# Shared keys of layer 1: their heads scaled on ScalarE, both cosine products ahead of both sums

## The chip, the cores and the metric

The kernel is one program on one core of a Trainium2 chip. The metric is the device time of one execution, in microseconds (us). Five engines work beside each other, each through its own queue, in program order: TensorE (PE in the rows; its weight loads are PEld), VectorE (DVE), ScalarE (ACT), GpSimd (POOL) and SyncE (SP), which only issues DMAs. They wait for each other by semaphores.

## What is computed

The reference is two transformer layers with a context stream, and then a block of another architecture. The change lies in the second layer (layer 1, the "odd" one), between the projection by `od_w_in` and its attention. Cut to what matters there:

```
p = a @ w_in                              # a: 256 latent and 256 context tokens
ck, cv, dk, dv = split(p_kv)              # ck: 2 heads of 64 shared by 8 query heads
ck = rms_norm(split_heads(ck, 2), ck_g)   # x * rsqrt(mean(x*x) + EPS) * g, per head
ck = apply_rope(ck, cos, sin)             # latent tokens only
out = window_gqa(cq, ck, cv, ck_ctx, cv_ctx, sink)   # attention, every query head needs all of ck
```

`window_gqa` is the first half of the attention stage, and `diff_attention_latent` (dq, dk, dv) the second.

## The kernel before, in words

Tokens lie in four tiles of 128: t = 0 and 1 are latent, t = 2 and 3 context. All float32 products are made of a high and a low half ("hi" and "lo"). A weight tile (128 x 2048) comes by DMA into a slot, ScalarE writes its high half (`feed` in the ScalarE program, line 1610), VectorE its low half (`feed` in the VectorE program, line 2212), and TensorE reads both (lines 933 to 935, three matmuls for each product).

The projection of the shared keys and values gives one bank of PSUM for each of the four token tiles, `("od", "ckv", t)`, with keys in columns 0 to 127 (two heads) and values in columns 128 to 255. For each key tile these steps follow:

1. ScalarE squares it (`odd_square`, line 1876).
2. VectorE sums the squares by head and makes the mean (`odd_means`, lines 2376 and 2289).
3. GpSimd raises it to the power -1/2 (`rsqrt`, line 3403).
4. VectorE scales the two heads with it (`odd_scale` to `head_scale`, line 2384): event `hn`.
5. For t = 0 and 1 VectorE makes the cosine product (line 2819), GpSimd the sine product (line 3480, event `orp`), and VectorE adds both (line 2836, event `orot`). For t = 2 and 3 there is only VectorE's product with the gain (line 2824, event `orot`).
6. TensorE turns the tile (`head_turn`, line 939), ScalarE writes the high half (line 1665, `ohi`), VectorE the low half (line 2284, `olo`).

The value half of the bank is copied by ScalarE (`odd_value`, line 1881, event `cv2`), which also gives the bank free. Before that copy ScalarE waits for `hn` of the tile.

The order on each engine is written by hand:

- ScalarE: the four squares; one exponential of two numbers for the lambda of the differential heads (line 1921, the first exponential after many Silu); then values and high halves of the keys in turn, `odd_value(0)`, `odd_value(1)`, `odd_hi(0)`, `odd_value(2)`, `odd_hi(1)`, and so on. `odd_hi(0)` feeds a weight tile first: the high half of the tile for the next pair of projections (`whi__62`). Then it squares the first pair, `dq`.
- VectorE: means 0; means 1, scale 0, rotate 0; means 2, scale 1, rotate 1; means 3, scale 2, rotate 2; scale 3, rotate 3; the four low halves of the keys; means of the pair `dq`; the low half of that weight tile (`wlo__61`).
- GpSimd: power 0, sine product 0, power 1, sine product 1, power 2, power 3.
- TensorE: 16 steps of the paired projections (`paired`), turns the four key tiles, then starts the attention stage `attend("a1")`: the scores of a head (lines 1191 to 1193), followed by more steps of the paired projections. Every unit of this stage waits for `ohi` and `olo` of all four key tiles and for all four values.

The scratch tiles of the change: `XN` (scaled keys, `odd__179` and `odd__180` in the rows), `XR` (`odd__181` to `184`), `XT` (sine products, `odd__185` and `186`), `SQ` (squares, `odd__187` and `188`), `CV` (values, `odd__172`), `CK3` (halves of the keys, `odd__170` and `171`). `XN`, `XT` and `SQ` have two buffers each, so tile t + 2 waits for tile t.

Of the kernel before, what the change touches and what calls it, by code (L numbers as in the profile page):

```python
# [15 lines left out]
ACT = mybir.ActivationFunctionType  # L16
# [104 lines left out]
class Count:  # L121
# [18 lines left out]
    "norm_a": ("nsq", "xn_a", "ntm_a", "nhi", "msq", "mxn", "mxh", "mx_a", "r0", "upon"),  # L140
    "root": ("nrs", "hrs", "lrs", "mrs", "prs"),
    "head_v": ("hrd", "hms", "hn", "qg", "qlo", "ocos", "orot", "olo", "dv_v", "v_v"),
    "head_a": ("hsq", "qhi", "ohi", "cv2", "dv_a", "v_a"),
    "conv_v": ("cu", "cw", "cv", "clo"), "conv_a": ("cg", "chi"),
    "att_v": ("neg", "pmix", "ptc_v", "fw", "fy", "flo"), "att_a": ("exp", "ptc_a", "fwe", "fhi"),
    "mod_v": ("grow", "spr", "stq_lo", "msum", "gsum", "gcp"), "mod_a": ("silu", "stq_hi", "cb"),
# [13 lines left out]
class Book:  # L160
# [6 lines left out]
    def did(self, name, *key, by=1):  # L167
        sem = SEM_OF.get(name, name)
        self.now[sem] += by
        if self.counting and not self.repeat:  # L170
            assert (name, *key) not in self.at, (name, key)
            assert self.by.setdefault(sem, self.engine) == self.engine, (name, sem)
            self.at[name, *key] = sem, self.now[sem]
        assert self.at[name, *key] == (sem, self.now[sem]), (name, key)
        return self.sems.get(sem), by
# [109 lines left out]
def _build(nc, ctx, I, cst_d, scr_d, out_d, packed):  # L285
    W = {name: Weight(name, SHAPES[name]) for name in WEIGHTS}
    book = Book()
    did = book.did
# [115 lines left out]
    XN, XR, XT, SQ = A3.some(2, 512), A3.some(4, 512), A3.some(2, 512), A3.some(2, 512)  # L404
# [90 lines left out]
    def bank(*key):  # L495
        return PS[bank_of[key]]
# [11 lines left out]
    SSN = [SM[:, 80 + 8 * i:88 + 8 * i] for i in range(8)]  # L508
# [72 lines left out]
    ODD_UNITS = [("cq", 0), ("cq", 1), *[("ckv", t) for t in range(4)], *PAIRS[0:6]]  # L581

    rotated = {("orp", *key) for key in ODD_UNITS if (key[2] == 0 if len(key) == 3 else key[1] < 2)}

    def turned_kind(kind, *at):
        return ("ck" if kind == "ckv" else kind, *at)
# [1011 lines left out]
    def scalar_program(e):  # L1598
        at = dict(tile=0, due=Due(book), gate="", ahead=2, slots={0, 1, 2, *slot_e})

        def due(*events):
            return at["due"](*events)
# [247 lines left out]
        for blk in range(2):  # L1850
            for f0 in range(0, 11, 2):
                m = min(2, 11 - f0)
# [17 lines left out]
        def odd_square(*key):  # L1870
            w_ = 128 if key[0] == "ckv" else 512
            feed(("prod", "od", *key))
            c = ODD_UNITS.index(key)
            for s, n in due(("prod", "od", *key), *([("hrd", *ODD_UNITS[c - 2])] if c > 1 else normed_lo("o", 1))):
                e.wait_ge(s, n)
            e.activation(SQ[c % 2][:, 0:w_], bank("od", *key)[:, 0:w_], ACT.Square).then_inc(*did("hsq", *key))

        def odd_value(t):
            for s, n in due(("hn", "ckv", t)):
                e.wait_ge(s, n)  # L1880
            e.activation(CV[:, t, :], bank("od", "ckv", t)[:, 128:256], ACT.Copy).then_inc(*did("cv2", t))
            empties(("od", "ckv", t), ("cv2", t))
# [27 lines left out]
        for t in range(2):  # L1910
# [3 lines left out]
            for o in range(2):  # L1914
                r = slice(64 * o, 64 * o + 64)
                e.activation(CQ4[t][r, :, o, :], v3(bank("ht", "cq", t), 4)[r], ACT.Copy).then_inc(*did("ohi", "cq", t, o))
        for t in range(4):
            odd_square("ckv", t)
        for s, n in due(("lam_s",)):
            e.wait_ge(s, n)  # L1920
        e.activation(LM[:, 2:4], LM[:, 0:2], ACT.Exp).then_inc(*did("lam_e"))
# [159 lines left out]
        for n_ in range(6):  # L2081
# [5 lines left out]
            for t in range(2):  # L2087
                if n_ >= 4:
                    if t:
                        for s, n in due(("prod", "s", n_, t), ("nrs", "s", t)):  # L2090
                            e.wait_ge(s, n)
                        e.activation(VA[:, t, (n_ - 4) * 384:(n_ - 3) * 384], bank("s", n_, t)[:, 0:384], ACT.Copy,
                                     scale=SS[:, t:t + 1]).then_inc(*did("sv_a", n_, t))
                        empties(("s", n_, t), ("sv_a", n_, t))
                    continue
                c = 2 * n_ + t
                for s, n in due(("prod", "s", n_, t), ("nrs", "s", t),
# [3 lines left out]
                             scale=SS[:, t:t + 1]).then_inc(*did("sx", n_, t))  # L2101
# [20 lines left out]
        for hf in range(2):  # L2122
            for t in range(2):
                feed(("prod", "uq", hf, t))
                for s, n in due(("prod", "uq", hf, t), ("score", "a2", 23, 0)):
                    e.wait_ge(s, n)
                m = e.activation(QTMS[t][:, hf * 384:(hf + 1) * 384], bank("uq", hf, t)[:, 0:384], ACT.Copy,
                                 scale=96 ** -0.5)
# [43 lines left out]
        for f0 in range(0, 32, 2):  # L2172
            c = f0 // 2
# [8 lines left out]
        past = []  # L2182
        for t in range(2):
            for half in range(2):
                post_square("mlp", half, t, bank("mlp2", t, half), JK, 16, ("prod", "mlp2", t, half), *past)
                past = [("psq", "mlp", half, t)]


    def vector_program(e):
        at = dict(tile=0, due=Due(book), gate="", chain=0, ahead=2, sums=0, slots={0, 1, 2, *slot_e}, begun=None, owed=[])  # L2190

        def due(*events):
            return at["due"](*events)
# [509 lines left out]
        for half in range(2):  # L2703
# [4 lines left out]
            for t in range(4):  # L2708
                feed(("prod", "o", 0, half, t))
                c = half * 4 + t  # L2710
# [36 lines left out]
        for blk in range(2):  # L2747
            for f0 in range(0, 11, 2):
                m = min(2, 11 - f0)
# [42 lines left out]
        def odd_means(*key):  # L2792
            w_, nh, c, _ = odd_unit(*key)
            head_means(key, nh, 64, SQ[c % 2], SSN[c % 8])

        def odd_scale(*key):
            w_, nh, c, (xn, _, _) = odd_unit(*key)
            past = [("orot", *turned_kind(*ODD_UNITS[c - 2]))] if c > 1 else [*normed_lo("o", 1)]
            head_scale(key, bank("od", *key)[:, 0:w_], nh, 64, SSN[c % 8], xn, ("prod", "od", *key), *past)
            if key[0] != "ckv":  # L2800
                empties(("od", *key), ("hn", *key))

        def odd_rotate(*key):
            odd_cosine(*key)
            odd_sum(*key)

        def odd_cosine(*key):
            w_, nh, c, (xn, xr, xt) = odd_unit(*key)
            g = dict(cq=0, ckv=1, dq=2, dk=3)[key[0]]
            heads = lambda x: x.rearrange("p (h f) -> p h f", f=64)  # L2810
            wide = lambda x, n: x.rearrange("p (o f) -> p o f", o=1).broadcast_to([128, n, 64])
            past = [("ht", *turned_kind(*ODD_UNITS[c - 4]))] if c > 3 else []
            for s, n in due(("hn", *key), ("tab",), *past):
                e.wait_ge(s, n)
            if ("orp", *key) in rotated:
                pair = range(2) if len(key) == 3 else (key[1],)
                for o, t in enumerate(pair):
                    x = slice(o * w_ // len(pair), (o + 1) * w_ // len(pair))
                    m = e.tensor_tensor(heads(xr[:, x]), heads(xn[:, x]),
                                        wide(TC[:, (g * 2 + t) * 64:(g * 2 + t) * 64 + 64], nh // len(pair)), ALU.mult)  # L2820
                m.then_inc(*did("ocos", *key))
            elif key[0] == "ckv":
                gain_ = GAIN[:, g * 64:(g + 1) * 64].rearrange("p (a o f) -> p a o f", a=1, o=1).broadcast_to([128, 2, 2, 64])
                e.tensor_tensor(twice(XR[c % 4]), spread_heads(xn), gain_, ALU.mult).then_inc(*did("orot", *turned_kind(*key)))
            else:
                e.tensor_tensor(heads(xr), heads(xn), wide(GAIN[:, g * 64:(g + 1) * 64], nh),
                                ALU.mult).then_inc(*did("orot", *turned_kind(*key)))
# [62 lines left out]
        for t in range(2):  # L2890
# [3 lines left out]
                low("olo", ("cq", t, o), CQ4[t][other, :, o, :], v3(bank("ht", "cq", t), 4)[r], CQ4[t][r, :, o, :],  # L2894
                    ("ohi", "cq", t, o))
            empties(("ht", "cq", t), ("olo", "cq", t, 1))
        for t in range(5):
            if t < 4:
                odd_means("ckv", t)
            if t:  # L2900
                odd_scale("ckv", t - 1)
                odd_rotate("ckv", t - 1)
        at["ahead"] = 0
        for t in range(4):
            odd_lo("ck", t, CK3, 2)
# [23 lines left out]
        for t, k0 in ((0, 0), (1, 4)):  # L2929
            for s, n in due(("mt", k0), ("gain", "n2b", 0), ("prod", "o", 1, 1, 1)):  # L2930
                e.wait_ge(s, n)
            for k in (k0, k0 + 1):
                m = e.tensor_scalar(XT32[:, k, :], bank("mt", k0)[:, (k - k0) * 256:(k - k0) * 256 + 256],
                                    sc2b[:, 2 * k:2 * k + 1], None, ALU.mult)
# [3 lines left out]
        for t in range(2):  # L2938
            for s, n in due(("router", t), ("mrs", t), ("r0",)):
                e.wait_ge(s, n)  # L2940
            m = e.scalar_tensor_tensor(out=LG[:, t * 8:t * 8 + 8], in0=bank("router", t)[:, 0:8], scalar=SS[:, t:t + 1],
                                       in1=R0, op0=ALU.mult, op1=ALU.add)
# [8 lines left out]
        for t in range(2):  # L2951
            m = e.max(MX[:, eight(t)], LG[:, eight(t)])
# [11 lines left out]
        for t in range(2):  # L2964
            m = e.tensor_scalar(SELR[:, eight(t)], iot, one(IX, t, 0), None, ALU.is_equal)
# [3 lines left out]
        for t in range(2):  # L2969
            m = e.scalar_tensor_tensor(out=SELR[:, eight(t)], in0=iot, scalar=one(IX, t, 1), in1=SELM[:, eight(t)],  # L2970
                                       op0=ALU.is_equal, op1=ALU.add)
# [208 lines left out]
        for n_ in range(6):  # L3180
# [5 lines left out]
            for t in range(2):  # L3186
# [8 lines left out]
                c = 2 * n_ + t  # L3195
# [169 lines left out]
    def gpsimd_program(e):  # L3365
# [99 lines left out]
        for c, key in enumerate(ODD_UNITS):  # L3465
            w_, g = (128, 1) if key[0] == "ckv" else (512, dict(cq=0, dq=2, dk=3)[key[0]])
            for c_, unit in [(0, ODD_UNITS[0]), (1, ODD_UNITS[1])] if c == 0 else [(c, key)] if c > 1 else []:
                rsqrt("hrs", unit, SSN[c_ % 8][:, 0:w_ // 64], ("hms", *unit))
            if ("orp", *key) in rotated:
                pair = range(2) if len(key) == 3 else (key[1],)  # L3470
                for s, n in due(("hn", *key), ("tab",)):
                    e.wait_ge(s, n)
                for o, t in enumerate(pair):
                    x = slice(o * w_ // len(pair), (o + 1) * w_ // len(pair))
                    nh = w_ // len(pair) // 64
                    x4 = XN[c % 2][:, x].rearrange("p (h q r f) -> p h q r f", h=nh, q=2, r=2)
                    t4 = XT[c % 2][:, x].rearrange("p (h q r f) -> p h q r f", h=nh, q=2, r=2)
                    for r in range(2):
                        tab = TS5[:, g, t, :, r, :].rearrange("p (o q) f -> p o q f", o=1).broadcast_to([128, nh, 2, 16])
                        m = e.tensor_tensor(t4[:, :, :, r, :], x4[:, :, :, 1 - r, :], tab, ALU.mult)  # L3480
                m.then_inc(*did("orp", *key))
# [142 lines left out]
```

## Time and profile before

| what | us |
|---|---|
| median of 3 runs | 1751.19 |
| lowest and highest | 1749.59 and 1753.67 |
| the profiled execution | 1750.59 |
| its span by the profile | 1748.8 |
| TensorE busy | 1649.5 |
| VectorE busy | 1233.2 |
| ScalarE busy | 835.9 |
| GpSimd busy | 163.5 |

The rows further below are of one profiled execution, with times from the start of its span. A row of a timeline has the start, the duration of the group, the engine, the line of the kernel, the operation, output and inputs with shapes, the count, and in brackets how long the engine had been idle before it and what is held to have released it. A short idle time can be named after the wrong engine where two ended at nearly the same moment. The granted clock of TensorE ("PEclk") is 1.00 at 2.4 GHz and 0.50 at 1.2 GHz.

### The profile page before, as it was taken

To read this page: it belongs to the slowest core of one execution; us is meant where nothing else is said; L and a number is where in the kernel's file an instruction comes from. 1 tells how busy PE (TensorE), PEld (TensorE's weight loads), DVE (VectorE), ACT (ScalarE), POOL (GpSimd) and SP (SyncE) were. 2 spreads that over 40 slices of the span, in tenths; PEclk is the share of its full clock that TensorE was granted. 3 is DMA by queue.
4 is the path that set the end of the run, shared out by engine and by line. 5 is a ranking of instruction groups with operands and counts; after the bars stand their busy time and mean duration, and the time that the engine had idled before them with its cause. 6 is when DMAs were issued, how large, how long until landed. Compare 5 with 4: busy or idle time off the path is not lost. (4 is left out here: it accounts for less than half of the span.)

```text
span 1748.8 us, 21453 instructions
## 1 busy us (share of the span) xinstructions
PE 1649.5 (94%) x8697; PEld 1405.3 (80%) x8697; DVE 1233.2 (71%) x1598; ACT 835.9 (48%) x1023; POOL 163.5 (9%) x157
## 2 busy tenths in 40 slices
PE   5999999999999999799899999999889989889998
PEld 2778877888888888697788788888779878779986
DVE  6488864587575545776689888998977666766644
ACT  6444433322122315344567777677655444555532
POOL 2110102000210023410200000002300000000000
PEclk9999989999999999898999999999999999999999
DMA  8443433355565423211479898898866622245553
GB/s 335 111 168 122 146 120 121 142 196 197 224 237 193 166 104 102 73 49 49 169 254 345 299 374 316 320 355 300 299 239 206 216 69 101 89 152 185 179 193 119
DMA packets 60505, 333.61 MB, mean 191 GB/s; under 512 B 14690, under 2 KB 15009, under 8 KB 28400
## 3 DMA queue, kind: packets, MB, share of 16 engines
q1 hardware_dynamic: 54640, 311.06, 49.0%
q0 software_dynamic: 4032, 14.57, 2.7%
q10 hardware_dynamic: 1728, 6.54, 1.0%
q8 instruction: 72, 1.18, 0.3%
q14 instruction: 33, 0.27, 0.0%
HBM read 331.00 MB, written 1.13 MB: 190 GB/s over the span
## 5 line engine op out<-in xcount | busy, mean ns | idle before, releaser
L2212 DVE TENSOR_TENSOR wlo__61<-raw__60,whi__62 128x2048 fp32r<-128x2048 f32 (+2 forms) x64 | 144.1, 2252 | 71.8 <-ACT whi__62 L1610 71.6
L2212 DVE TENSOR_TENSOR wlo__65<-raw__64,whi__66 128x2048 fp32r<-128x2048 f32 (+3 forms) x64 | 139.8, 2185 | 64.8 <-ACT whi__66 L1610 64.8
L1610 ACT ACTIVATE whi__62<-raw__60 128x2048 fp32r<-128x2048 f32 (+2 forms) x64 | 119.0, 1859 | 91.3 <-DMA raw__60<-in_ffn_w 43.1
L1610 ACT ACTIVATE whi__66<-raw__64 128x2048 fp32r<-128x2048 f32 (+3 forms) x64 | 115.4, 1803 | 70.7 <-DMA raw__64<-in_ffn_w 31.0
L2212 DVE TENSOR_TENSOR wlo__69<-raw__68,whi__70 128x2048 fp32r<-128x2048 f32 (+4 forms) x50 | 109.2, 2183 | 23.9 <-ACT whi__70 L1610 23.9
L3403 POOL TENSOR_TENSOR keep__58<-keep__58,keep__59 128x1 f32<-128x1 f32 (+3 forms) x48 | 53.4, 1116 | 601.8 <-DVE keep__58 L2289 601.7
L2248 DVE SCALAR_TENSOR_TENSOR wsum__71<-raw__68,silu_rows 128x1024 f32<-128x1024 f32 x84 | 100.0, 1220 | 1.4 <-DMA raw__68<-in_ada_w 0.8
L1610 ACT ACTIVATE whi__70<-raw__68 128x2048 fp32r<-128x2048 f32 (+4 forms) x50 | 90.5, 1810 | 17.1 <-DMA raw__68<-in_w_ff 11.8
L2212 DVE TENSOR_TENSOR wlo__237<-raw__236,whi__238 128x2048 fp32r<-128x2048 f32 (+1 forms) x24 | 51.3, 2138 | 10.1 <-ACT whi__238 L1610 9.9
L2508 DVE TENSOR_REDUCE keep__58<-ps 128x1 f32<-128x256 f32 (+1 forms) x88 | 44.5, 517 | 13.6 <-PE ps L1194 4.9
L2212 DVE TENSOR_TENSOR wlo__233<-raw__232,whi__234 128x2048 fp32r<-128x2048 f32 (+1 forms) x24 | 50.5, 2106 | 1.8 <-ACT whi__234 L1610 1.7
L933 PE MATMUL ps<-ffn__129,wlo__61 128*128 128x512 f32 (+1 forms) x128 | 47.5, 371 | 4.4 <-DVE ffn__130 L2284 2.7
L935 PE MATMUL ps<-ffn__129,whi__62 128*128 128x512 f32 (+1 forms) x128 | 47.0, 367 | 0.0
L934 PE MATMUL ps<-ffn__130,whi__62 128*128 128x512 f32 (+1 forms) x128 | 47.0, 367 | 0.0
L1610 ACT ACTIVATE whi__234<-raw__232 128x2048 fp32r<-128x2048 f32 (+1 forms) x24 | 42.5, 1771 | 8.5 <-DMA raw__232<-in_moe_w 8.4
L2248 DVE SCALAR_TENSOR_TENSOR wsum__147<-raw__144,silu_rows 128x1024 f32<-128x1024 f32 x36 | 44.3, 1251 | 0.4
L3501 POOL TENSOR_TENSOR moe__212<-moe__212,keep__57 128x512 f32<-128x512 f32 x2 | 11.4, 5686 | 351.2 <-DVE moe__213 L3077 343.6
L2212 DVE TENSOR_TENSOR wlo__241<-raw__240,whi__242 128x2048 fp32r<-128x2048 f32 (+2 forms) x24 | 43.2, 1798 | 1.2 <-ACT whi__242 L1610 1.2
L933 PE MATMUL ps<-ffn__129,wlo__141 128*128 128x512 f32 x112 | 43.6, 389 | 0.0
L934 PE MATMUL ps<-ffn__130,whi__142 128*128 128x512 f32 x112 | 43.6, 389 | 0.0
L935 PE MATMUL ps<-ffn__129,whi__142 128*128 128x512 f32 x112 | 43.6, 389 | 0.0
L933 PE MATMUL ps<-ffn__129,wlo__65 128*128 128x512 f32 x112 | 43.6, 389 | 0.0
(1173 smaller groups left out, 5331.0 us busy)
## 6 DMA issues: line engine op xcount, KB each, us to landing
raw__68<-in_moe_w SPq DMA_DIRECT2D x24, 1024.0 KB, 5.4
raw__60<-in_moe_w SPq DMA_DIRECT2D x24, 1024.0 KB, 5.7
raw__68<-in_ada_w SPq DMA_DIRECT2D x16, 1024.0 KB, 4.9
raw__64<-in_moe_w SPq DMA_DIRECT2D x16, 1024.0 KB, 5.5
raw__232<-in_moe_w SPq DMA_DIRECT2D x16, 1024.0 KB, 6.6
raw__236<-in_moe_w SPq DMA_DIRECT2D x16, 1024.0 KB, 7.2
raw__144<-in_ada_w SPq DMA_DIRECT2D x13, 1024.0 KB, 6.2
raw__68<-in_ada_w POOLq DMA_DIRECT2D x20, 512.0 KB, 4.1
```

The costliest lines, as they stand in the source:

```text
L933: e.matmul(out, ll, rh, start=start, stop=False)
L934: e.matmul(out, lh, rl, start=False, stop=False)
L935: return e.matmul(out, lh, rh, start=False, stop=stop)
L1610: e.activation(t.hi(), t.raw(), ACT.Copy).then_inc(*did("hi", i))
L2212: e.tensor_tensor(t.lo(), t.raw(), t.hi().bitcast(F32), ALU.subtract).then_inc(*did("lo", i))
L2248: m = e.scalar_tensor_tensor(out=junk, in0=slot_raw[t.slot][:, c * 1024:c * 1024 + 1024], scalar=1.0, in1=CB[:, v * D:(v + 1) * D], op0=AL ...
L2508: m = e.tensor_reduce(neg, b[:, 0:u.total], AX.X, ALU.max, negate=True)
L3403: e.tensor_tensor(x, x, EXPO[:, 0:1].broadcast_to([128, n_]) if n_ > 1 else EXPO[:, 0:1], ALU.pow).then_inc(*did(out, *key))
L3501: e.tensor_tensor(MACC[t][:, hs], MACC[t][:, hs], GBC[:, gs], ALU.mult).then_inc(*did("hgate", t, half))
```

## The change

ScalarE scales the heads of the four shared key tiles, one activation with a scale from memory for each head of 64 columns, in place of VectorE's one instruction for both. The scaled event is now `hna`, on ScalarE; VectorE's and GpSimd's products wait for it, and so does the copy of the values. On ScalarE the four scalings stand among the four squares, and thus ahead of the exponential at line 1921 and of all that follows it. On VectorE the order becomes: means 0, means 1, cosine 0, cosine 1, sum 0, means 2, sum 1, means 3, and the two products with the gain. GpSimd's and TensorE's order stays.

```diff
-    "head_a": ("hsq", "qhi", "ohi", "cv2", "dv_a", "v_a"),
+    "head_a": ("hsq", "hna", "qhi", "ohi", "cv2", "dv_a", "v_a"),
...
+    def head_normed(*key):
+        return ("hna" if key[0] == "ckv" else "hn", *key)
...
+        def odd_scale(t):
+            c = ODD_UNITS.index(("ckv", t))
+            for s, n in due(("hrs", "ckv", t), ("prod", "od", "ckv", t), ("orot", *turned_kind(*ODD_UNITS[c - 2]))):
+                e.wait_ge(s, n)
+            for h in range(2):
+                x = slice(h * 64, h * 64 + 64)
+                m = e.activation(XN[c % 2][:, x], bank("od", "ckv", t)[:, x], ACT.Copy, scale=SSN[c % 8][:, h:h + 1])
+            m.then_inc(*did("hna", "ckv", t))
+
         def odd_value(t):
-            for s, n in due(("hn", "ckv", t)):
+            for s, n in due(("hna", "ckv", t)):
...
-        for t in range(4):
-            odd_square("ckv", t)
+        for t in range(5):
+            if t < 4:
+                odd_square("ckv", t)
+            if t:
+                odd_scale(t - 1)
         for s, n in due(("lam_s",)):
             e.wait_ge(s, n)
         e.activation(LM[:, 2:4], LM[:, 0:2], ACT.Exp).then_inc(*did("lam_e"))
...
-            for s, n in due(("hn", *key), ("tab",), *past):
+            for s, n in due(head_normed(*key), ("tab",), *past):
...
-        for t in range(5):
-            if t < 4:
-                odd_means("ckv", t)
-            if t:
-                odd_scale("ckv", t - 1)
-                odd_rotate("ckv", t - 1)
+        for t in range(2):
+            odd_means("ckv", t)
+        for t in range(2):
+            odd_cosine("ckv", t)
+        for t in range(2):
+            odd_sum("ckv", t)
+            odd_means("ckv", 2 + t)
+        for t in range(2, 4):
+            odd_cosine("ckv", t)
...
-                for s, n in due(("hn", *key), ("tab",)):
+                for s, n in due(head_normed(*key), ("tab",)):
```

## Rows read from the trace of the kernel before

**Rows 1.** The page's first part: busy time, share, instructions of each engine.

```profile
PE 1649.5 (94%) x8697; PEld 1405.3 (80%) x8697; DVE 1233.2 (71%) x1598; ACT 835.9 (48%) x1023; POOL 163.5 (9%) x157
```

**Rows 2.** Windows: stretch, length, busy (instructions) of PE, PEld, DVE, ACT, POOL, clock, DMA.

```profile
713.30:716.50 3.20, 0.73 (x2) 0.30 (x2) 3.12 (x4) 0.48 (x1) 2.21 (x1) 0.60 0.00 0
716.50:720.80 4.30, 4.25 (x20) 4.28 (x21) 3.09 (x8) 0.83 (x3) 3.29 (x5) 0.50 0.02 4
...
806.00:809.00 3.00, 2.61 (x11) 2.29 (x13) 2.01 (x6) 1.94 (x5) 0.00 (x0) 0.52 0.02 5
...
815.00:818.00 3.00, 3.00 (x16) 2.43 (x15) 2.25 (x5) 1.21 (x4) 0.00 (x0) 0.78 0.13 52
```

**Rows 3.** The timeline of TensorE at the start of the attention stage.

```profile
708.10 0.41 PE L939 MATMUL ps<-keep__49,odd__183 128*128 128x128 f32 x2
709.92 0.44 PE L939 MATMUL ps<-keep__49,odd__184 128*128 128x128 f32 x2 [1.42 <-DVE odd__184 L2836]
...
713.40 0.47 PE L1191 MATMUL ps<-odd__171,odd__164 128*128 128x512 f32 x1 [1.02 <-ACT odd__187 L1876]
...
716.55 0.55 PE L933 MATMUL ps<-whi__62,odd__175 128*128 128x256 f32 x1 [2.42 <-DVE wlo__61 L2212]
```

**Rows 4.** The timeline of ScalarE in the same stretch.

```profile
705.81 0.28 ACT L1876 ACTIVATE odd__188<-ps 128x128 f32<-128x128 f32 x1
706.11 1.28 ACT L1921 ACT_TABLE_LOAD   x1
...
707.51 0.26 ACT L1881 ACTIVATE odd__172<-ps 128x128 f32<-128x128 f32 x1
...
708.76 1.90 ACT L1610 ACTIVATE whi__62<-raw__60 128x2048 fp32r<-128x2048 f32 x1
710.56 0.38 ACT L1665 ACTIVATE odd__170<-ps 128x256 fp32r<-128x256 f32 x1
710.83 0.28 ACT L1881 ACTIVATE odd__172<-ps 128x128 f32<-128x128 f32 x1
710.98 0.40 ACT L1665 ACTIVATE odd__170<-ps 128x256 fp32r<-128x256 f32 x1
...
712.42 0.38 ACT L1665 ACTIVATE odd__170<-ps 128x256 fp32r<-128x256 f32 x1 [0.46 <-PE ps L939]
712.70 0.59 ACT L1876 ACTIVATE odd__187<-ps 128x512 f32<-128x512 f32 x1
```

**Rows 5.** The timeline of VectorE in the same stretch.

```profile
706.34 0.29 DVE L2384 TENSOR_TENSOR odd__179<-ps,keep__58 128x128 f32<-128x128 f32 x1 [0.42 <-POOL keep__58 L3403]
...
707.53 0.42 DVE L2836 TENSOR_TENSOR odd__183<-odd__183,odd__185 128x256 f32<-128x256 f32 x1 [0.56 <-POOL odd__185 L3480]
707.87 0.28 DVE L2376 TENSOR_REDUCE keep__58<-odd__187 128x2 f32<-128x128 f32 x1
708.18 0.17 DVE L2289 TENSOR_SCALAR keep__58<-keep__58 128x2 f32<-128x2 f32 x1
...
711.40 0.42 DVE L2824 TENSOR_TENSOR odd__182<-odd__180,odd__159 128x256 f32<-128x256 f32 x1
711.74 1.51 DVE L2284 TENSOR_TENSOR odd__171<-ps,odd__170 128x256 fp32r<-128x256 f32 x4
713.32 0.69 DVE L2376 TENSOR_REDUCE keep__58<-odd__187 128x8 f32<-128x512 f32 x1
...
714.12 2.28 DVE L2212 TENSOR_TENSOR wlo__61<-raw__60,whi__62 128x2048 fp32r<-128x2048 f32 x1
```

**Rows 6.** The timeline of GpSimd in the same stretch.

```profile
705.61 0.70 POOL L3403 TENSOR_TENSOR keep__58<-keep__58,keep__59 128x2 f32<-128x2 f32 x1 [6.47 <-DVE keep__58 L2289]
706.72 0.71 POOL L3480 TENSOR_TENSOR odd__185<-odd__179,odd__161 128x64 f32<-128x64 f32 x2 [0.41 <-DVE odd__179 L2384]
```

**Rows 7.** Groups of instructions by line, 650 to 800: an activation with a pointer, one without.

```profile
L1689 ACT ACTIVATE keep__50<-ps,keep__58 128x512 f32<-128x512 f32 x8 | 5.5, 688 | 21.8 <-DVE keep__58 L2506 21.8
...
L1665 ACT ACTIVATE odd__168<-ps 128x512 fp32r<-128x512 f32 x4 | 2.4, 598 | 0.0
```

## The prediction

> **What bounds the kernel now.** I read the page's busy line first: TensorE is busy for 1649.5 of the span's 1748.8 us [rows 1], so a change elsewhere counts only where it moves an idle time of TensorE. The windows show such a place beside the change: from 713.3 to 716.5 TensorE is busy for 0.73 of 3.20 us, and from 716.5 on it is busy at the low clock, 0.50 [rows 2]. The timeline of TensorE says what it waits for [rows 3]. It turns the first key tile at 708.10, right behind its projections, without a wait; the second at 709.92; its first scores begin at 713.40; the paired projections go on at 716.55, released by VectorE's `wlo__61`. So three times matter: when the fourth key tile's low half ends (711.74 + 1.51 = 713.25 [rows 5], the scores 0.15 later), when `wlo__61` ends (714.12 + 2.28 = 716.40 [rows 5], the matmul 0.15 later), and what is ahead of these two.
>
> `wlo__61` stands behind VectorE's sum of the squares of `dq` at 713.32, and that began 0.03 us after ScalarE's square of `dq` had ended (712.70 + 0.59 = 713.29 [rows 4, 5]). The low half of the last key tile needs its high half, ScalarE's row at 712.42, which had waited 0.46 us for TensorE's turn of that tile; that turn needs VectorE's product of 711.40 to 711.82 [rows 4, 5]. In this kernel, then, the chain into the attention stage is VectorE's chain of the four tiles, and ScalarE has its work done ahead of it: the load of the activation table for the exponential ran from 706.11 to 707.39, the high half `whi__62` from 708.76 to 710.66 [rows 4], both while VectorE and GpSimd were still on tiles 0 to 2. These two, 3.1 us of ScalarE, are covered now. My reading is that the change takes the cover away.
>
> **The change part by part: the scaled heads.** Removed from VectorE are four scalings, 0.29 us each [rows 5], 1.2 us in all. Added to ScalarE are four pairs of activations over 64 columns. No such row is in the trace. From above: an activation over 128 columns of PSUM takes 0.28 and one over 256 takes 0.38 [rows 4], so 64 columns take about 0.23; the scale from memory costs more, by the exponential with one pointer (688 ns over 512 columns) against the copy without (598 ns) [rows 7], 0.09 to 0.10. That gives 0.33 for one and, with the overlap of neighbours (710.56 + 0.38 against the next start, 710.83: 0.11 [rows 4]), 0.55 for a pair. From below, without the pointer's cost, a pair takes 0.36. I take 0.55, since the exponentials are the nearer row.
>
> **The chain of the four tiles.** Handing over costs 0.03 us (GpSimd's power ends at 706.31, VectorE starts at 706.34) to 0.09 (VectorE's scaling ends at 706.63, GpSimd starts at 706.72) [rows 5, 6]; I take 0.06 into ScalarE and 0.03 out of it to VectorE, 0.08 to GpSimd. Power 0 ends at 706.31 as now. Scaling 0 runs 706.37 to 706.92, GpSimd's sine product (0.71) 707.00 to 707.71, power 1 (0.69 to 0.70, overlapping by 0.04) to 708.36, scaling 1 to 708.97, cosine product 1 (0.29) from 709.01 to 709.30. Only now comes VectorE's sum 0, at about 709.22 where it now is at 707.53: it is queued behind a cosine product that waits for tile 1. The sum takes 0.34 to the next start and the mean 0.49 (707.87 to 708.35 [rows 5]): mean 2 ends at 710.05, sum 1 starts at 709.97, mean 3 ends at 710.80. Power 3 runs 710.88 to 711.58, scaling 3 711.64 to 712.19, and VectorE's last product 712.22 to 712.64, where it now ends at 711.82. By VectorE's side alone the change would cost 0.8 us. The 1.2 us taken from VectorE are no gain, since that engine waits for powers and products of GpSimd in this stretch (idle 0.42 and 0.56 us before two of its rows [rows 5]).
>
> **What is queued behind scaling 3 on ScalarE.** In the new order the exponential, its table load, the four value copies, `whi__62` and the four high halves all stand behind the last scaling. From its end, 712.19: 0.02 to the table load (square 705.81 + 0.28, load at 706.11), 1.40 from the load to the first value copy (706.11 to 707.51), four value copies at 0.15 to the next start (710.83 to 710.98), 0.60, `whi__62` 1.80 (708.76 to 710.56), and four high halves at 0.27 or 0.28 (710.56 to 710.83; 712.42 to 712.70), 1.09 [rows 4]. That is 4.91 us, and the square of `dq` starts at 717.10, where it now starts at 712.70: 4.40 us later. The last high half moves by the same 4.4, to 716.8, and with it the low half, the first scores (713.40 to 717.8) and `wlo__61` (714.12 to 718.5), and the paired projections (716.55 to about 720.95). VectorE, out of work from 712.6 to about 715.7, can't make up for it: both of its next steps need ScalarE's.
>
> Turning the third and fourth key tile now also waits, since these turns take the banks of the shared keys and values 0 and 1, which are free only after their value copies, at about 713.8. This is hidden: the high halves are not due before 716. GpSimd's order is as before, and no DMA is issued by a moved step. The weight tile asked for at the end of TensorE's last projection, 708.2, stays where it is.
>
> **Where the 4.4 us go.** After this point each of TensorE, VectorE, ScalarE and GpSimd goes on from an event that is later by the same amount, and the loads of the attention stage and of the experts behind it are issued when TensorE has consumed an older tile, so they shift too. I find no wait in that stage that a later start would fill up: none of its waits names a transfer of weights before the experts. The shift should reach the end whole. From the profiled execution, 1750.59 us, it gives 1755.0; that execution is 0.6 below the median, and from the median, 1751.19, it is **1755.6**. With pairs of 0.36 instead of 0.55 the chain ends some 0.5 us sooner (three of the four lie on it) and the shift is 3.9; with GpSimd's sine product slowed beside VectorE's sum, at worst by that sum's 0.42 us [rows 5], it is 4.8.
>
> **A rule against the trace.** The row of the table load ends at 707.39 and a value copy starts at 707.51, with only the small exponential between them [rows 4]; nothing else of that size stands beside the load. The Trainium skill ("ScalarE: Activation LUTs", section "What ACT_TABLE_LOAD costs") gives about 1283 ns for the load, as here, and about 1380 ns more for draining at every switch. The trace does not show that second part: the load started 0.02 us after the square before it. By the page's sum the shift would be 5.8 us, and I keep it as a rival. The same page has the compiler place the load right before the activation that needs it; by that the load moves with the exponential, behind the scalings, which is also the order that my sum took from the row's line number, 1921.
>
> **The rivals.**
>
> *VectorE's side alone (1752.0, chance 0.08).* ScalarE's tail would not end last, or part of it (`whi__62`) stands elsewhere than I read it. Then 0.8 us remain. Against it: all scores need all four high halves, and of the 4.9 us behind scaling 3 only 0.5 run beside VectorE's last product.
>
> *The table load goes ahead of the scalings (1754.3, chance 0.07).* ScalarE has to wait for power 0 anyway, so there the load would cost little. The shift is then 4.4 - 1.28 = 3.1. Against it: the load's row has the line of the exponential.
>
> *The drain (1757.0, chance 0.04).* A switch of tables that comes right behind two activations costs 1.4 us more than this trace shows.
>
> *The clock, on the other side (1750.5, chance 0.12).* The granted clock falls after idle time of TensorE and comes back while it is busy. From 806 to 818, in four windows of which the first and last stand here, it was 0.52, 0.50, 0.50 and 0.78 [rows 2], that is 10.2 us at 0.50 under a nearly always busy TensorE. Work of 10.2 us at half clock takes 5.1 at full. If the later start puts that fall elsewhere or avoids it, 5.1 us come back: 1755.6 - 5.1 = 1750.5. It decides from 8.8 us less at the low clock. For it: such falls depend on short idle times. Against it: the idle time that precedes is of the stage's own making and shifts with it. The stretch of 716.5 to 720.8 at 0.50 [rows 2] I expect to stay, moved to 721 to 725.
>
> *One low stretch more (1757.8, chance 0.09).* The longer gap ahead of 720.95, or a new fall in the stage, adds some 4.5 us at the low clock, 2.2 us.
>
> **How the numbers follow.** The forecast has 0.60, with a range of its own of 1754.2 to 1756.6 from the bounds above and the spread of the medians. About 0.2% of the time, 3.5 us, is what a measurement of this kernel can tell from no change; the bound is at 1754.7. Most of the forecast (0.47 of 0.60), the drain and the added stretch are slower by more; the rest of the forecast, VectorE's side, the early load and the clock are within; faster by more takes two avoided stretches, 0.04, taken from the clock's 0.12. So slower 0.60, same 0.36, faster 0.04. The range leaves out some of the two ends: 1750.8 to 1757.6.
>
> **What would show it.** In the changed kernel ScalarE's table load should start near 712.2 and not 706.1, `whi__62` near 713.9, the square of `dq` near 717.1; TensorE's first scores near 717.8 and the projections near 721.0; VectorE idle for some 3 us before its four low halves; GpSimd's fourth power near 710.9. Each pair of scalings should take 0.36 to 0.55 us. If the load is still at 706, the step on ScalarE's queue is wrong; if the scores start near 714, the step that ScalarE ends last is; if the shift at 721 is 4.4 and the end moves by less, the step that nothing behind absorbs it.

## The result and the profile after

| what | us |
|---|---|
| before, median of 20 runs | 1750.28 (1746.66 to 1753.67) |
| changed, median of 20 runs | 1753.49 (1751.23 to 1757.83) |
| ratio, 95% interval | 1.0017 (1.0010 to 1.0023) |
| the changed kernel's profiled execution | 1757.03, span 1755.2 |

The change makes the kernel 3.0 us slower by the ratio (1.8 to 4.0 by its interval). The span of the profiled execution is 6.4 us longer than before's, but 1.7 of these lie ahead of the change: VectorE's first mean of a key tile starts at 706.73 instead of 705.04. The rest is 4.4 us in the stretch shown here and 0.3 behind it. One execution of a later kernel, 2709 us at a mean granted clock of 0.56, is left out of all ratios. I therefore take 1.69 us off each time of the changed kernel when I compare it with a row of before. The row in the timeline of VectorE of the kernel before:

```profile
705.04 0.28 DVE L2376 TENSOR_REDUCE keep__58<-odd__187 128x2 f32<-128x128 f32 x1
```

And its last scaling, which the reading of ScalarE's rows below needs (it ends at 711.37):

```profile
711.08 0.29 DVE L2384 TENSOR_TENSOR odd__180<-ps,keep__58 128x128 f32<-128x128 f32 x1
```

ScalarE in the changed kernel, the rows that answer to [rows 4]; columns as there:

```profile
708.03 0.52 ACT L1887 ACTIVATE odd__179<-ps,keep__58 128x64 f32<-128x64 f32 x2 [1.89 <-POOL keep__58 L3421]
...
713.31 0.52 ACT L1887 ACTIVATE odd__180<-ps,keep__58 128x64 f32<-128x64 f32 x2
713.84 1.28 ACT L1936 ACT_TABLE_LOAD   x1
715.13 0.20 ACT L1936 ACTIVATE odd__162<-odd__162 128x2 f32<-128x2 f32 x1
715.25 0.43 ACT L1893 ACTIVATE odd__172<-ps 128x128 f32<-128x128 f32 x2
715.56 1.91 ACT L1613 ACTIVATE whi__62<-raw__60 128x2048 fp32r<-128x2048 f32 x1
717.36 0.38 ACT L1668 ACTIVATE odd__170<-ps 128x256 fp32r<-128x256 f32 x1
...
718.20 0.70 ACT L1668 ACTIVATE odd__170<-ps 128x256 fp32r<-128x256 f32 x2
718.73 0.66 ACT L1879 ACTIVATE odd__187<-ps 128x512 f32<-128x512 f32 x1
```

The last scaling ends at 713.83 and the square of `dq` starts at 718.73: 4.90 us without a gap. Before, only 1.33 us lay between these two points (711.37 to 712.70); the rest of ScalarE's work was done beside VectorE's chain, ahead of the last scaling. The load of the table moved from 706.11 to 713.84 - 1.69 = 712.15.

VectorE in the changed kernel, the rows that answer to [rows 5]:

```profile
706.73 0.29 DVE L2391 TENSOR_REDUCE keep__58<-odd__187 128x2 f32<-128x128 f32 x1
...
710.58 0.29 DVE L2834 TENSOR_TENSOR odd__184<-odd__180,odd__160 128x128 f32<-128x128 f32 x1 [1.70 <-ACT odd__180 L1887]
710.79 0.54 DVE L2851 TENSOR_TENSOR odd__183<-odd__183,odd__185 128x256 f32<-128x256 f32 x1
...
713.86 0.42 DVE L2839 TENSOR_TENSOR odd__182<-odd__180,odd__159 128x256 f32<-128x256 f32 x1 [0.24 <-ACT odd__180 L1887]
717.77 1.64 DVE L2299 TENSOR_TENSOR odd__171<-ps,odd__170 128x256 fp32r<-128x256 f32 x4 [3.49 <-ACT odd__170 L1668]
719.42 0.69 DVE L2391 TENSOR_REDUCE keep__58<-odd__187 128x8 f32<-128x512 f32 x1
720.14 0.17 DVE L2304 TENSOR_SCALAR keep__58<-keep__58 128x8 f32<-128x8 f32 x1
720.22 2.29 DVE L2227 TENSOR_TENSOR wlo__61<-raw__60,whi__62 128x2048 fp32r<-128x2048 f32 x1
```

VectorE's last product ends at 714.28, and then the engine stands for 3.49 us until ScalarE's first high half. Before, the low halves followed the last product at once.

TensorE in the changed kernel, the rows that answer to [rows 3]:

```profile
715.56 0.69 PE L942 MATMUL ps<-keep__49,odd__181 128*128 128x128 f32 x2 [3.01 <-ACT odd__172 L1893]
...
719.56 0.76 PE L1194 MATMUL ps<-odd__171,odd__164 128*128 128x512 f32 x1 [2.88 <-DVE odd__171 L2299]
...
722.65 0.55 PE L936 MATMUL ps<-whi__62,odd__175 128*128 128x256 f32 x1 [1.91 <-DVE wlo__61 L2227]
```

The third key tile waits 3.01 us for a bank, which ScalarE's copy of the values (`odd__172`) sets free; this wait is hidden, as the high halves come only at 717.36. The scores wait for the low halves, the projections for `wlo__61`.

The same stretch and the next in windows of the changed kernel, the rows that answer to [rows 2]; columns: stretch, length, busy (instructions) of PE, PEld, DVE, ACT, POOL, clock, DMA share and GB/s:

```profile
715.50:719.50 4.00, 1.12 (x4) 0.72 (x4) 1.69 (x5) 4.00 (x11) 0.00 (x0) 0.50 0.00 2
719.50:722.60 3.10, 1.19 (x2) 0.50 (x2) 3.04 (x4) 0.38 (x1) 2.21 (x1) 0.50 0.00 0
722.60:727.00 4.40, 4.35 (x20) 4.38 (x21) 3.16 (x8) 0.93 (x3) 3.29 (x5) 0.50 0.01 4
```

From 715.5 to 719.5 ScalarE is busy for 4.00 of 4.00 us and TensorE for 1.12: the engine with 48% of the span busy is the one that the kernel waits for here. A stretch at the low clock stands behind the restart as before, but it is longer than the window shown: the clock is 0.50 from 727.0 to 728.5 too and 0.99 from 728.5 to 732.0, so it lasts 5.9 us from the restart, where before's lasted 4.2. A second profile of the same changed kernel (the last run below) has 2.9 us there, so the change does not set this length.

### The profile page after: what moved, and what is told of

The parts are those of the page before. It is cut to its first block and busy times, and to the rows that moved or that the text cites. A ratio compares the mean times of both kernels' runs of the same rounds, so it can differ in the third digit from the quotient of the medians.

```text
span 1755.2 us, 21456 instructions
## 1 busy us (share of the span) xinstructions
PE 1650.0 (94%) x8697; PEld 1405.8 (80%) x8697; DVE 1231.5 (70%) x1594; ACT 837.4 (48%) x1031; POOL 162.2 (9%) x157
## 5 line engine op out<-in xcount | busy, mean ns | idle before, releaser
L2263 DVE SCALAR_TENSOR_TENSOR wsum__71<-raw__68,silu_rows 128x1024 f32<-128x1024 f32 x84 | 100.0, 1220 | 1.8 <-DMA raw__68<-in_ada_w 1.2
L936 PE MATMUL ps<-ffn__129,wlo__141 128*128 128x512 f32 x112 | 43.7, 390 | 0.9 <-issue 0.9
L937 PE MATMUL ps<-ffn__130,whi__142 128*128 128x512 f32 x112 | 43.6, 389 | 0.0
L938 PE MATMUL ps<-ffn__129,whi__142 128*128 128x512 f32 x112 | 43.6, 389 | 0.0
L936 PE MATMUL ps<-ffn__129,wlo__65 128*128 128x512 f32 x112 | 43.6, 389 | 0.0
L937 PE MATMUL ps<-ffn__130,whi__66 128*128 128x512 f32 x112 | 43.6, 389 | 0.0
```

Of the source, the lines that this page charges most:

```text
L936: e.matmul(out, ll, rh, start=start, stop=False)
L937: e.matmul(out, lh, rl, start=False, stop=False)
L938: return e.matmul(out, lh, rh, start=False, stop=stop)
L2263: m = e.scalar_tensor_tensor(out=junk, in0=slot_raw[t.slot][:, c * 1024:c * 1024 + 1024], scalar=1.0, in1=CB[:, v * D:(v + 1) * D], op0=AL ...
```

## The experiments

Each run is read by one number from its trace, here called the stretch: from the start of VectorE's first mean of a key tile to the restart of the paired projections on TensorE. It leaves out what lies ahead, which differs by up to 3.9 us between the twelve profiles (the first mean starts between 702.87 and 706.73). In each profile these are the first `TENSOR_REDUCE` of 128x2 and the first matmul with `whi__62` behind the scores. The time over before is the ratio of the runs less one, times 1751 us, with its 95% interval.

| kernel | stretch, us | over before's | time over before, us |
|---|---|---|---|
| before | 11.51 | | |
| changed | 15.92 | 4.41 | 3.0 (1.8 to 4.0) |
| changed, again | 15.95 | 4.44 | 3.9 (2.1 to 5.4) |
| exponential ahead | 14.40 | 2.89 | 1.6 (-0.2 to 3.3) |
| exponential and weight tile ahead | 12.61 | 1.10 | -0.7 (-2.3 to 0.9) |
| VectorE's old order | 15.67 | 4.16 | 2.5 (0.9 to 4.0) |
| before with ScalarE's tail behind | 15.22 | 3.71 | 4.0 (1.8 to 6.3) |
| before with VectorE's new order | 11.85 | 0.34 | 0.2 (-1.4 to 1.8) |
| two more table loads | 18.95 | 7.44 | 6.0 (3.7 to 8.2) |
| all means first | 10.95 | -0.56 | -3.0 (-4.6 to -1.4) |
| power 2 between the sine products | 10.39 | -1.12 | -2.3 (-3.9 to -0.9) |
| eight tiny copies | 11.77 | 0.26 | 0.7 (-0.7 to 2.3) |

The stretch still holds a part of TensorE's clock. In the profiles of "VectorE's new order" and "eight tiny copies" the clock fell to 0.50 before TensorE turned the last key tile, in before's only after it. The last turn in before, with eight tiny copies, and with the new order:

```profile
711.97 0.41 PE L939 MATMUL ps<-keep__49,odd__182 128*128 128x128 f32 x2 [0.49 <-ACT odd__170 L1665]
...
710.39 0.66 PE L939 MATMUL ps<-keep__49,odd__182 128*128 128x128 f32 x2 [0.24 <-DVE odd__182 L2826]
...
712.17 0.66 PE L939 MATMUL ps<-keep__49,odd__182 128*128 128x128 f32 x2
```

It takes 0.66 us instead of 0.41 and lies on the path to the restart, so some 0.25 us of these two stretches are the clock's. Differences of a quarter of a microsecond from before's 11.51 say nothing about an edit by themselves.

### The exponential ahead of the scalings

```diff
-        for t in range(5):
-            if t < 4:
-                odd_square("ckv", t)
-            if t:
-                odd_scale(t - 1)
+        for t in range(2):
+            odd_square("ckv", t)
         for s, n in due(("lam_s",)):
             e.wait_ge(s, n)
         e.activation(LM[:, 2:4], LM[:, 0:2], ACT.Exp).then_inc(*did("lam_e"))
+        for t in range(4):
+            odd_scale(t)
+            if t < 2:
+                odd_square("ckv", t + 2)
```

> The changed kernel with one move: the exponential for lambda, and so its table load, stands right behind the second square, ahead of the scalings. I read the stretch from VectorE's first mean of a key tile to the restart of the paired projections; it was 11.51 us before (705.04 to 716.55) and 15.92 after (706.73 to 722.65), 4.4 more. Theory Q (ScalarE's queue behind the last scaling): the load runs while ScalarE waits for the first power, 1.4 us leave the tail, the stretch is 14.5 and the time some 1.4 us under the changed kernel's. Theory C (the four-tile chain of VectorE and GpSimd with slower scalings is what costs): the stretch stays 15.9.

Measured: stretch 14.40 (14.5 expected), ratio 1.0009 (0.9999 to 1.0019). ScalarE's rows of this kernel:

```profile
701.65 1.28 ACT L1933 ACT_TABLE_LOAD   x1
702.94 0.20 ACT L1933 ACTIVATE odd__162<-odd__162 128x2 f32<-128x2 f32 x1
704.17 0.52 ACT L1887 ACTIVATE odd__179<-ps,keep__58 128x64 f32<-128x64 f32 x2 [1.02 <-POOL keep__58 L3422]
```

The load ends, and ScalarE still waits 1.02 us for the first power: the load is hidden there, and 1.52 us have left the stretch. Where the load stands in the queue is thus a third of the local cost, and theory C, in which ScalarE's queue plays no part, is out.

### The weight tile ahead too

```diff
         for t in range(4):
             odd_scale(t)
             if t < 2:
                 odd_square("ckv", t + 2)
+            if t == 1:
+                feed(("ht", "ck", 0))
```

> As the run before, and the high half of the weight tile stands behind the second scaling instead of behind the value copies. Theory Q: another 1.8 us leave the tail, the stretch from VectorE's first mean to the restart of the projections is 12.7 (1.2 over before's), the time within 1.5 us of before. Theory C: still 15.9 and 3 us over before.

Measured: stretch 12.61 (12.7 expected), ratio 0.9996 (0.9987 to 1.0005). With both ahead the change costs 1.1 us in the stretch and nothing that can be measured in the time. It is no gain either: taking four instructions from VectorE buys nothing here.

### ScalarE's tail behind the last scaling, in the kernel before

```diff
-        for s, n in due(("lam_s",)):
+        for s, n in due(("lam_s",), ("hn", "ckv", 3)):
```

> The kernel before, scalings on VectorE in the old order, with one wait added: ScalarE waits for the last scaled keys before the exponential for lambda. No scaling is moved; only ScalarE's tail (table load, value copies, high half of the weight tile, high halves of the keys) begins behind the last scaling, at 711.4. Theory Q: the square of dq starts 4.9 us later, at 716.3 by the clock of the trace before, the stretch is 15.1 (3.6 over before's 11.5), the time some 3 us over before. Theory C: stretch and time as before.

Measured: stretch 15.22 (15.1 expected), ratio 1.0023 (1.0010 to 1.0036). ScalarE's rows of this kernel:

```profile
705.19 0.28 ACT L1876 ACTIVATE odd__188<-ps 128x128 f32<-128x128 f32 x1
710.83 1.28 ACT L1921 ACT_TABLE_LOAD   x1 [5.36 <-DVE odd__180 L2384]
712.12 0.20 ACT L1921 ACTIVATE odd__162<-odd__162 128x2 f32<-128x2 f32 x1
```

This is the run that decides. No scaling is moved and VectorE's order is the old one; one wait sends the same tail behind the last scaling, and 3.71 of the 4.41 us are there. ScalarE idles for 5.36 us and the load begins at the end of that wait: the load doesn't use the idle time, as it stands behind the wait of its own activation.

### VectorE's old order with scalings on ScalarE, and the new order alone

```diff
-        for t in range(2):
-            odd_means("ckv", t)
-        for t in range(2):
-            odd_cosine("ckv", t)
-        for t in range(2):
-            odd_sum("ckv", t)
-            odd_means("ckv", 2 + t)
-        for t in range(2, 4):
-            odd_cosine("ckv", t)
+        for t in range(5):
+            if t < 4:
+                odd_means("ckv", t)
+            if t:
+                odd_rotate("ckv", t - 1)
```

> The changed kernel with VectorE's old order (mean, rotate in turn), so only the scalings are on ScalarE. Theory Q: the last scaling ends 0.2 us sooner, since mean 2 no longer stands behind a product that waits for tile 1, and all else follows: the stretch is 15.7 and the time as the changed kernel's. Theory C, with VectorE's new order as the cost: the stretch falls by 0.8 or more.

Measured: stretch 15.67 (15.7 expected), ratio 1.0014 (1.0005 to 1.0023). The other half of the change, in the kernel before:

```diff
+        for t in range(2):
+            odd_means("ckv", t)
+        for t in range(2):
+            odd_scale("ckv", t)
+            odd_cosine("ckv", t)
+        for t in range(2):
+            odd_sum("ckv", t)
+            odd_means("ckv", 2 + t)
+        for t in range(2, 4):
+            odd_scale("ckv", t)
+            odd_cosine("ckv", t)
```

> The kernel before with only VectorE's order changed: means 0 and 1, then scaling and cosine product of tiles 0 and 1, then sum 0, mean 2, sum 1, mean 3, then the context tiles; scalings stay on VectorE, ScalarE's order is the old one. Worked out from the rows of before: VectorE's last product ends within 0.1 us of 711.8, so the stretch from the first mean to the restart of the projections is 11.5 and the time is that of before. A theory that the order of VectorE costs by itself expects 12.3.

Measured: stretch 11.85, 0.3 more than expected, ratio 1.0001 (0.9992 to 1.0010). VectorE's last product in this kernel:

```profile
711.60 0.42 DVE L2824 TENSOR_TENSOR odd__182<-odd__180,odd__159 128x256 f32<-128x256 f32 x1
```

It ends 6.87 us after the first mean (712.02 - 705.15), in before 6.78 (711.82 - 705.04). With the scalings on VectorE the order thus costs 0.09 us, as expected, and the other 0.25 of the 0.34 are the last turn at the low clock. With the scalings on ScalarE it costs 0.25 (15.92 - 15.67), where the last turns are hidden and the clock plays no part. Neither could be seen in the time.

### Two more table loads

```diff
+        e.activation(LM[:, 5:6], LM[:, 0:1], ACT.Exp)
+        e.activation(LM[:, 6:7], LM[:, 0:1], ACT.Silu)
         e.activation(LM[:, 2:4], LM[:, 0:2], ACT.Exp).then_inc(*did("lam_e"))
```

> The changed kernel with two more table loads and two more tiny activations right behind the one that is there (an exponential, a Silu, then the exponential for lambda; their results are not read). Theory Q, with nothing behind that absorbs: 2 x 1.28 + 2 x 0.11 = 2.8 us more in the tail, the stretch is 18.7, and the time is 2.8 over the changed kernel's. If something behind absorbs part of a shift (the measured 3.2 us against 4.4 in the stretch), the time rises by only 2.0. If draining costs 1.4 us at a switch, as a rule has it, the stretch is 21.5.

Measured: stretch 18.95, ratio 1.0034 (1.0021 to 1.0047). ScalarE's rows of this kernel:

```profile
712.84 1.28 ACT L1936 ACT_TABLE_LOAD   x1
714.13 0.20 ACT L1936 ACTIVATE odd__162<-odd__162 128x1 f32<-128x1 f32 x1
714.34 1.28 ACT L1937 ACT_TABLE_LOAD   x1
715.64 0.20 ACT L1937 ACTIVATE odd__162<-odd__162 128x1 f32<-128x1 f32 x1
715.85 1.28 ACT L1938 ACT_TABLE_LOAD   x1
```

One more load with its activation costs 1.50 us (712.84 to 714.34 to 715.85), where I had 1.39: the activation ahead of a load ends before the load starts, so its 0.20 us count whole, and not the 0.11 or 0.12 to the start of the next activation. Both together are 3.0, as the stretch has it (18.95 - 15.95). The drain of the prediction, 1.4 us more at each switch, is not in these rows: each load starts 0.01 us after the activation before it has ended, and the next activation 0.01 or 0.02 us after the load.

### A shorter chain in the kernel before

```diff
-        for t in range(5):
-            if t < 4:
-                odd_means("ckv", t)
-            if t:
-                odd_scale("ckv", t - 1)
-                odd_rotate("ckv", t - 1)
+        for t in range(4):
+            odd_means("ckv", t)
+        for t in range(2):
+            odd_scale("ckv", t)
+            odd_cosine("ckv", t)
+        for t in range(2):
+            odd_sum("ckv", t)
+            odd_scale("ckv", 2 + t)
+            odd_cosine("ckv", 2 + t)
...
-            for c_, unit in [(0, ODD_UNITS[0]), (1, ODD_UNITS[1])] if c == 0 else [(c, key)] if c > 1 else []:
+            powers = {0: (0, 1), 2: (2, 3), 4: (4, 5)}.get(c, (c,) if c > 5 else ())
+            for c_, unit in [(c_, ODD_UNITS[c_]) for c_ in powers]:
```

> The kernel before, scalings on VectorE, with VectorE's four means first and GpSimd's order power 0, power 1, sine product 0, sine product 1, power 2, power 3. The chain of powers and products is then shorter: the last product ends near 710.6 instead of 711.8, and ScalarE's tail is ahead of it, so the stretch is 10.3 and the time up to 1.2 us under before.

Measured: stretch 10.95, ratio 0.9983 (0.9974 to 0.9992). The stretch is 0.65 longer than expected. VectorE's rows of this kernel say why:

```profile
706.95 0.54 DVE L2836 TENSOR_TENSOR odd__183<-odd__183,odd__185 128x256 f32<-128x256 f32 x1
708.35 0.29 DVE L2384 TENSOR_TENSOR odd__179<-ps,keep__58 128x128 f32<-128x128 f32 x1 [0.86 <-POOL keep__58 L3406]
```

Scaling 2 waits 0.86 us for power 2, which is queued behind both sine products on GpSimd. So power 2 was put between them:

```diff
-            powers = {0: (0, 1), 2: (2, 3), 4: (4, 5)}.get(c, (c,) if c > 5 else ())
+            powers = {0: (0, 1), 2: (2, 3), 3: (4,), 4: (5,)}.get(c, (c,) if c > 5 else ())
```

> As the kernel with all means first, but GpSimd's order is power 0, power 1, sine product 0, power 2, sine product 1, power 3. Power 2 then ends behind the first sine product, near the end of sum 0, so VectorE's last product ends about 0.5 us sooner than with both sine products ahead of power 2: the stretch from the first mean to the restart of the projections is 10.4 (10.95 there, 11.51 before), the time 1.1 us under before if the stretch alone counts, 3 under if the gain of that kernel (measured 0.17%) was of the order itself.

Measured: stretch 10.39 (10.4 expected), ratio 0.9987 (0.9978 to 0.9995). GpSimd's rows of this kernel:

```profile
704.01 1.36 POOL L3406 TENSOR_TENSOR keep__58<-keep__58,keep__59 128x2 f32<-128x2 f32 x2 [6.49 <-DVE keep__58 L2289]
705.50 0.71 POOL L3484 TENSOR_TENSOR odd__185<-odd__179,odd__161 128x64 f32<-128x64 f32 x2
706.17 0.74 POOL L3406 TENSOR_TENSOR keep__58<-keep__58,keep__59 128x2 f32<-128x2 f32 x1
706.89 0.59 POOL L3484 TENSOR_TENSOR odd__186<-odd__180,odd__161 128x64 f32<-128x64 f32 x2
```

GpSimd now goes from power to product with hardly a gap, where it used to wait for a mean and a scaling each time. Both kernels are faster than before and than the changed one. They gain where the change lost: on the chain that sets the scores, not on the engine that looked busy.

### The place in the queue

```diff
         paired(-1)
+        for i in range(8):
+            e.activation(LP[:, i:i + 1], LM[:, 0:1], ACT.Copy)
         attend("a1", paired)
```

> The kernel before with eight copies of one column added on ScalarE behind its squares of dq, where it is idle for 6.2 us (their results are not read); the stretch stays 11.5. It tells whether the place of later instructions, eight further on ScalarE's queue as in the changed kernel, moves the time by itself: the five kernels with scalings on ScalarE came out about 1.5 us under what their stretches say. Theory P (place in the queue): 1.5 us under before. Theory N (nothing but the spread of runs, or another cause): within 1 us of before.

Measured: stretch 11.77, ratio 1.0004 (0.9996 to 1.0013). In the trace the copies stand between the two squares of `dq` (711.84, 0.84 us for all eight) and not behind both, so the second square starts later; the restart doesn't wait for it. The 0.26 us in the stretch are the last turn at the low clock, as shown above. Eight further instructions on ScalarE's queue don't make the rest faster; theory P falls.

### The changed kernel again

> The changed kernel once more, beside new runs of before. If the end moves by what the stretch moves (4.4 us), the ratio is 1.0025; if 1.2 us are given back behind the stretch, it is 1.0018 as measured at first.

Measured: stretch 15.95, ratio 1.0022 (1.0012 to 1.0031), 3.9 us. It holds both answers: 4.4 us is within this interval, and so is 3.0.

## Why the prediction was right, and where not

**The local sum held, step by step.** Less 1.69 us, the rows after stand against the forecast as follows:

| step | forecast | measured |
|---|---|---|
| a pair of scalings, length | 0.55 | 0.52 |
| sum 0 starts | 709.22 | 709.10 |
| mean 3 ends | 710.80 | 710.77 |
| scaling 3 ends | 712.19 | 712.14 |
| table load starts | 712.2 | 712.15 |
| `whi__62` starts | 713.9 | 713.87 |
| square of `dq` starts | 717.10 | 717.04 |
| first scores | 717.8 | 717.87 |
| projections restart | 720.95 | 720.96 |

The forecast shift was 4.40 us and the stretch grew by 4.41. It is made of 0.77 us by which the last scaling ends later (712.14 against 711.37), 3.57 more between it and the square of `dq` (4.90 against 1.33), and 0.07 from there to the restart. What made it so near is that each row of ScalarE's tail is an instruction that the trace of before had already timed; only the scalings were new, and they are 0.5 us each.

**The rivals.** The run that only sends the tail behind the last scaling shows the cause by itself, 3.71 us, so VectorE's side alone is out. The table load didn't go ahead of the scalings: it moved with its exponential, in every kernel where that was moved. There is no drain in the rows. Of the 0.8 us on the chain of the four tiles VectorE's order has 0.25 and the longer scalings 0.52: with the old order the last product ends 7.30 us after the first mean, with the new one 7.55, in before 6.78. The low clock of 716.5 to 720.8 is there again behind the restart, as forecast, but with 5.9 us in one profile of the changed kernel and 2.9 in the other, against 4.2. GpSimd's sine product was slowed beside VectorE's sum, by which I had widened the range: the second one took 0.89 us instead of 0.71. It is off the path, as the last powers wait for VectorE's means.

**The end moved by less than the stretch, and this step is not settled.** I forecast that all 4.4 us reach the end. The first comparison has 3.0 with an upper end of 4.0, which leaves 4.4 out; the second has 3.9, up to 5.4. Over all eleven comparisons with before, a line through stretch against time has the slope 0.98 (standard error 0.11): within that error a microsecond here is a microsecond at the end. But the line lies 1.0 us under the origin (standard error 0.4), and the first comparison 1.4 us under its own stretch. Two kernels with hardly any shift (new order alone, tiny copies) and the one with the tail behind lie within 0.5 us of the stretch, the others 0.5 to 2.4 under. Some 0.25 us of this may be before's own stretch, which is longer by so much in an execution whose clock falls early. The place of instructions in ScalarE's queue is not the reason, by the run of tiny copies.

The profiles point to the clock for a part of the rest. The rival of the clock named the stretch of 806 to 818, of which 10.2 us were at 0.50 in before. The same place in the changed kernel:

```profile
808.00:811.00 3.00, 2.49 (x11) 1.52 (x10) 2.01 (x6) 1.45 (x4) 0.00 (x0) 0.91 0.00 0
811.00:814.00 3.00, 2.03 (x10) 1.63 (x9) 2.61 (x5) 0.91 (x3) 0.00 (x0) 0.50 0.02 5
814.00:817.00 3.00, 3.00 (x14) 1.93 (x14) 2.33 (x7) 1.02 (x3) 0.29 (x1) 0.50 0.00 0
817.00:820.00 3.00, 2.70 (x20) 1.99 (x18) 1.98 (x6) 1.45 (x4) 0.78 (x2) 0.95 0.04 12
```

These are 6.8 us at 0.50. The four profiles with the whole tail behind scalings on ScalarE (changed, changed again, old order, two more loads) have 6.8 there too. And from the restart to ScalarE's next table load (889.25 in before, 896.66 in the changed kernel) they take 173.4 to 174.0 us, where seven of the other eight profiles take 175.0 to 175.6. So some 1.5 us come back in the attention stage, about what is missing. Three things keep this from being shown: before's own profile takes 172.7, the kernel with the tail behind has 6.8 us at the low clock there as well and takes 175.2, and the kernels with the exponential ahead, with the weight tile ahead and with the new order of powers also lie 1.2 to 2.4 us under their stretches though this stage is not shorter in them. No run here sets the clock by itself. It stays open.

**Size and sign.** The forecast from the median, 1755.6, is 2.1 over the measured 1753.49. Of these, 0.9 are before's own median, which was 1751.19 over 3 runs and 1750.28 over 20; the other 1.2 are the step just told. By the bound that I gave, 3.5 us, the result lies just on the side of the same, where I had 0.36, and not on the side of slower, 0.60. The sign is clear of noise. The wide range of 1750.8 to 1757.6 held; the forecast's own range, 1754.2 to 1756.6, did not. By its size alone the result is nearer to the rival in which the table load goes ahead (1754.3) than to the forecast, so it is the rows, and not the time, that tell the two apart.

## What to carry to other kernels

Before work is moved to an engine because it is less busy, read what stands behind the new place in its queue: the price here was 4.4 us on the path, of which the scalings and VectorE's order were 0.8, and 3.6 were other work that had been done early and now waited with them (4.9 us behind the last scaling instead of 1.3). In these traces a table load is part of that queue and stands behind the waits of its activation; put the first activation of a new table where its engine must wait anyway. And where a chain goes over three engines, as here, a new order of VectorE's means and GpSimd's powers gave a gain (1.1 us in the stretch, 2.3 in the time) that the work taken from VectorE did not.

## What was not expected of the hardware

An activation ahead of a table load is not overlapped by it: two loads with their tiny activations took 1.50 us each, where the activation of 0.20 us that another activation follows (715.13 and 715.25) holds it up by only 0.12. A pair of activations over 64 columns each, with a scale from memory, took 0.52 us. The gain of the two kernels with the new order of powers, 3.0 and 2.3 us, is more than the 0.6 and 1.1 by which their stretches are shorter; for the second the interval (0.9 to 3.9) includes the stretch, for the first (1.4 to 4.6) it does not, and no run here says why.
